# The dense layers' up product by seven block products, with its sums on GpSimd

## The reference, cut to what matters

```python
def sqrelu_mlp(h, w1, w2):              # h (1, 512, 1024), w1 (1024, 4096), w2 (4096, 1024)
    u = jax.nn.relu(jnp.einsum('bsd,df->bsf', h, w1))
    return jnp.einsum('bsf,fd->bsd', u * u, w2)

for i in range(2):
    hn = rmsnorm(h, norm_mix[i])
    mix = conformer_conv(hn, ...) if i == 0 else pool_mixer(hn, ...)
    h = h + mix
    h = h + sqrelu_mlp(rmsnorm(h, norm_mlp[i]), mlp_w1[i], mlp_w2[i])
return rmsnorm(h, final_norm)
```

## Time and profile before

| What | Value |
|---|---|
| Median of 3 runs | 886.83 us (886.45 to 887.8) |
| Span of the profiled execution | 884.7 us |
| Granted TensorE clock | 0.999 of full speed |
| PE busy | 874.4 us (99%) |
| DVE busy | 700.1 us (79%) |
| ACT busy | 464.1 us (52%) |
| POOL busy | 140.0 us (16%) |
| SP's queue | 29.4% of the DMA engines' span |

### The profile page before, as it was taken

How to read it: one execution, slowest core, us unless ns; L and a number is a source line. 1 busy time by engine, 2 the same in 40 slices (tenths; PEclk the granted TensorE clock), 3 DMA queues, 4 the chain that set the end, 5 groups by cost and what they waited for, 6 DMA issues and landing times.

```text
span 884.7 us, 11889 instructions
## 1 busy us (share of the span) xinstructions
PE 874.4 (99%) x4383; PEld 740.7 (84%) x4383; DVE 700.1 (79%) x946; ACT 464.1 (52%) x675; POOL 140.0 (16%) x122
## 2 busy tenths in 40 slices
PE   8999999999999999999999999999999999999997
PEld 8888887899888888888888889988888888888886
DVE  6899999768786968776778788897786968776866
ACT  6898976247272544536273544637272544536243
POOL 1699970560000020000000040000000000000000
PEclk9999999999999999999999999999999999999999
DMA  9766732305413142331314222122313142331202
GB/s 302 198 166 150 188 73 98 143 1 191 143 47 143 57 175 77 118 133 57 142 48 167 77 73 90 48 98 94 142 47 142 52 174 77 125 127 64 72 1 95
DMA packets 49255, 97.62 MB, mean 110 GB/s; under 512 B 1562, under 2 KB 18978, under 8 KB 48324
## 3 DMA queue, kind: packets, MB, share of 16 engines
q1 hardware_dynamic: 48068, 89.54, 29.4%
q0 software_dynamic: 1008, 7.34, 4.0%
q10 hardware_dynamic: 144, 0.26, 0.1%
HBM read 87.70 MB, written 2.10 MB: 101 GB/s over the span
## 4 chain that ended last, share of the span: by engine, by line
PE 95%; DVE 2%; DMA 1%; ACT 1%; issue 0%; SPq 0%; DVEq 0%; ACTq 0%
PE ps L1454 19%; PE ps L1452 19%; PE ps L1453 19%; PE ps L1717 10%; PE ps L1715 10%; PE ps L1716 10%; PE ps L1530 3%; PE ps L1471 1%; PE ps L1629 1%; PE ps L1634 1%; PE ps L1630 1%; DMA h<-in_x 1%; DVE tok L894 0%; DVE act_lo L900 0%; DVE tok L928 0%
## 5 line engine op out<-in xcount | busy, mean ns | idle before, releaser
L1452 PE MATMUL ps<-act_hi,w_hi 128*128 128x512 f32 (+1 forms) x688 | 254.9, 370 | 0.0
L1453 PE MATMUL ps<-act_lo,w_hi 128*128 128x512 f32 (+1 forms) x688 | 254.2, 369 | 0.0
L1454 PE MATMUL ps<-act_hi,w_lo 128*128 128x512 f32 (+1 forms) x688 | 254.2, 369 | 0.0
L1715 PE MATMUL ps<-w_hi,u_hi 128*128 128x512 f32 x392 | 152.7, 390 | 0.0
L1717 PE MATMUL ps<-w_hi,u_lo 128*128 128x512 f32 x392 | 152.7, 390 | 0.0
L1716 PE MATMUL ps<-w_lo,u_hi 128*128 128x512 f32 x392 | 152.5, 389 | 0.0
L685 ACT ACTIVATE relu<-ps 128x512 f32<-128x512 f32 x36 | 21.5, 597 | 242.8 <-PE ps L1454 242.8
L1452 PEld LDWEIGHTS ps<-act_hi,w_hi 128*128 128x128 f32 x688 | 129.7, 188 | 21.8
L1454 PEld LDWEIGHTS ps<-act_hi,w_lo 128*128 128x128 f32 x688 | 129.6, 188 | 21.8
L1453 PEld LDWEIGHTS ps<-act_lo,w_hi 128*128 128x128 f32 x688 | 129.7, 188 | 21.7
L1172 DVE TENSOR_TENSOR w_lo<-w_raw,w_hi 128x1024 fp32r<-128x1024 f32 x70 | 85.1, 1220 | 58.0 <-ACT w_hi L706 58.0
(11 more groups left out here) (237 smaller groups left out, 1264.0 us busy)
## 6 DMA issues: line engine op xcount, KB each, us to landing
w_raw<-in_mlp_w SPq DMA_DIRECT2D x32, 1024.0 KB, 5.0
w_raw<-in_mlp_w SPq DMA_DIRECT2D x16, 2048.0 KB, 8.0
w_raw<-in_conv_w SPq DMA_DIRECT2D x16, 512.0 KB, 5.5
prod_a<-prod_a POOLq DMA_DIRECT2D x7, 1024.0 KB, 7.9
w_raw<-in_conv_w SPq DMA_DIRECT2D x2, 2048.0 KB, 11.0
h<-in_x SPq DMA_DIRECT2D x4, 512.0 KB, 5.8
out<-tok SPq DMA_DIRECT2D x7, 256.0 KB, 2.0
gain<-in_norm_mlp SPq DMA_DIRECT2D x2, 512.0 KB
```

Source lines behind the costliest of these rows:

```text
L1452: nc.tensor.matmul(dst, lh, rh, start=(n == 0), stop=False)
L1453: nc.tensor.matmul(dst, lh, rl, start=False, stop=False)
L1454: return nc.tensor.matmul(dst, ll, rh, start=False, stop=(n == count - 1))
L1715: nc.tensor.matmul(dst, lh, rh, start=(f == 0 and (opens or i not in (0, 5))), stop=False)
```

## The change

The up product of groups 1 to 7 is also done by seven block products. The 1024 channels, the 512 features of the group and the 512 tokens are each cut in two. Weight blocks w11, w21, w12, w22 (128 x 1024 elements per block: 4 channel chunks x 256 features) and four sums v1 to v4 of them give seven weight parts; the activation quarters and four sums z1 to z4 (formed once for a layer, eight steps) give seven right sides. A part is 2 feature tiles x 4 channel chunks x 3 = 24 matmuls of 256 columns. The seven products are put together by seven sums on DVE (sum_two to sum_21), each of one SBUF operand and one PSUM bank, into a11, a12, a21, a22 in SBUF, and relu and square then work in SBUF. ACT copies the first product out of PSUM (copy_one).

Where things are done: POOL forms t1 to t4 (b_sums), v1 to v4 (w_sums) and the activations' sums (mlp_sums), adds acc to h at a layer's end (acc_out), and makes pw_lo; all low parts of weights and activations are on DVE (w_low, mid_low, x_low). High parts stay on ACT. The loads of pool_scale and pool_w are moved behind load_groups(0), that of norm_mix[1] behind the last low part of the layer's activations. The last down product starts on two features' tiles and takes the other two after that.

```diff
--- before.py
+++ after.py
...
+        w_parts = (w11, v1, v2, w12, v3, v4, w22)
+        wp_hi = w1_hi[:].rearrange("p (k c f) -> p k c f", k=4, c=4)
+        wp_lo = w1_lo[:].rearrange("p (k c f) -> p k c f", k=4, c=4)
+        def act_quarter(half, pair):
+            return slice(4 * half, 4 * half + 4), slice(256 * pair, 256 * pair + 256)
+        x_hi = (x_sum[:, 0], x_two[:, 0], x_sum[:, 2], act_hi[:, 0:4, 256:512])
+        x_lo = (x_sum[:, 1], x_two[:, 1], x_sum[:, 3], act_lo[:, 0:4, 256:512])
+        x_parts = (x_raw[:, 1], tok[:, 1, :].rearrange("p (c t) -> p c t", c=4), x_raw[:, 3], act_raw[:, 0:4, 256:512])
+        z1, z2, z3, z4 = x_parts
...
+            def b_sums(layer, g, which, again=True):
+                sums, splits = LAYER_SUMS * layer, LAYER_SPLITS * layer
+                for k in which:
+                    if k == 0:
+                        pool.wait_ge(m2_in[0], 16 * g + 16 * (GROUPS * layer + 1))
+                        if again:
+                            pool.wait_ge(w2_lo_ok, 7 * g + (splits - 2))
+                        into, left, right = t1, b12, b11
+                    elif k == 1:
+                        pool.wait_ge(m2_in[1], 16 * g + 16 * (GROUPS * layer + 1))
+                        into, left, right = t3, b22, b12
+                    elif k == 2:
+                        if again:
+                            pool.wait_ge(w2_lo_ok, 7 * g + (splits - 1))
+                        into, left, right = t2, b22, t1
+                    else:
+                        pool.wait_ge(w2_lo_ok, 7 * g + (splits + 3))
+                        into, left, right = t4, t2, b21
+                    nc.gpsimd.tensor_tensor(into, left, right, ALU.subtract).then_inc(b_sum_ok, 1)
+                    pool.wait_ge(b_sum_ok, 4 * g + (sums + k + 1))
+            def w_sums(layer, g, which, again=True):
+                for k in which:
+                    if k == 0:
+                        pool.wait_ge(w1_in, 16 * g + (32, 16 * (GROUPS + 2))[layer])
+                        into, left, right, op = v3, w11, w21, ALU.subtract
+                    elif k == 1:
+                        if again:
+                            pool.wait_ge(w1_mid_lo_ok, mid_lows(layer, g) - 1)
+                        into, left, right, op = v2, w22, v3, ALU.subtract
+                    elif k == 2:
+                        pool.wait_ge(w1_lo_ok, first_low(layer, g) + 1)
+                        into, left, right, op = v1, v2, w11, ALU.add
+                    else:
+                        pool.wait_ge(w1_mid_lo_ok, mid_lows(layer, g) + 3)
+                        into, left, right, op = v4, w12, v2, ALU.subtract
+                    nc.gpsimd.tensor_tensor(into, left, right, op).then_inc(w_sum_ok, 1)
+                    pool.wait_ge(w_sum_ok, 4 * g + (LAYER_WSUMS * layer - 4 + k + 1))
...
+            def x_block(layer, k, into, half, pair):
+                cs, at = act_quarter(half, pair)
+                x_step(layer, k, into, act_hi[:, cs, at].bitcast(F32), act_lo[:, cs, at].bitcast(F32), ALU.add)
+            def mlp_sums(layer, gen):
+                nc.gpsimd.memset(acc[:], 0.0).then_inc(acc_zero, 1)
+                b_sums(layer, 0, (0, 1, 2), False)
+                pool.wait_ge(act_lo_ok, 4 * gen + NB)
+                x_block(layer, 1, z1, 1, 1)
+                x_block(layer, 2, z3, 0, 1)
+                x_step(layer, 3, z3, z1, z3, ALU.subtract)
+                b_sums(layer, 0, (3,))
+                x_block(layer, 4, z2, 0, 0)
+                x_step(layer, 5, z2, z3, z2, ALU.add)
+                x_step(layer, 6, z1, z1, z2, ALU.subtract)
+                pool.wait_ge(up_mm, LAYER_PARTS * layer + GF)
+                x_block(layer, 7, z4, 1, 0)
+                x_step(layer, 8, z4, z4, z2, ALU.subtract)
+                w_sums(layer, 1, (0, 1, 2), False)
+                w_sums(layer, 1, (3,))
+                b_sums(layer, 1, (0, 1))
+                with pool.Fori(1, MIDDLE - 1) as w:
+                    b_sums(layer, w, (2, 3))
+                    w_sums(layer, w + 1, (0, 1, 2))
+                    w_sums(layer, w + 1, (3,))
+                    b_sums(layer, w + 1, (0, 1))
+                b_sums(layer, MIDDLE - 1, (2, 3))
+                w_sums(layer, MIDDLE, (0, 1, 2))
+                w_sums(layer, MIDDLE, (3,))
+            def acc_out(layer):
+                pool.wait_ge(banks_read, layer + 1)
+                tiles = ((h[:, 2:4, 512:D], acc[:, 0]), (h[:, 0:2, 512:D], acc[:, 0]),
+                         (h[:, 2:4, 0:512], acc[:, 1]), (h[:, 2:4, 512:D], acc[:, 1]))
+                for k, (at, add) in enumerate(tiles):
+                    if k == 3:
+                        pool.wait_ge(acc_out_ok, 4 * layer + 1)
+                    nc.gpsimd.tensor_tensor(at, at, add, ALU.add).then_inc(acc_out_ok, 1)
+            mlp_sums(0, GEN_MLP0)
+            acc_out(0)
...
+            pool.wait_ge(pw_hi_ok, 1)
+            pool.wait_ge(acc_out_ok, 4)
+            nc.gpsimd.tensor_tensor(pw_lo[:], pw_raw, pw_hi[:].bitcast(F32), ALU.subtract).then_inc(pw_lo_ok, 1)
...
+            mlp_sums(1, GEN_MLP1)
+            acc_out(1)
...
+            def w_part(i):
+                nc.scalar.copy(wp_hi[:, i % 4], w_parts[i]).then_inc(w1_hi_ok, 1)
+            def next_parts(layer, g):
+                act.wait_ge(w_sum_ok, 4 * g + (LAYER_WSUMS * layer - 4 + 3))
+                w_part(1)
+                w_part(2)
+                w_part(3)
+            def copy_one(layer, g):
...
-                    relu_square(n, UP_BANK[0], squared[0][:, 0], upper_b)
-                    next_w1(0)
-                    relu_square(n + 1, UP_BANK[1], squared[0][:, 1], diff_b)
-                    act.wait_ge(usq_ok, n + 2)
+                    act.wait_ge(m_done, 14 * w + (tiles - 4))
+                    upper_b()
+                    copy_one(layer, w)
+                    late_parts(layer, w, (4, 5))
+                    diff_b()
+                    late_parts(layer, w, (6,))
+                    lower_b()
+                    act.wait_ge(up_sum_ok, summed + 3)
+                    relu_square(n, a11, a11)
+                    act.wait_ge(usq_ok, n + 1)
-                    lower_b()
+                    act.wait_ge(up_sum_ok, summed + 5)
+                    relu_square(n + 1, a22, a22)
+                    act.wait_ge(up_sum_ok, summed + 6)
+                    relu_square(n + 2, a21, a21)
+                    last_b()
                     act.wait_ge(a_sum_ok, 4 * w + (sums + 1))
                     a_high(1)
-                    next_w1(1)
...
+                    act.wait_ge(up_sum_ok, summed + 7)
+                    relu_square(n + 3, a12, a12)
+                    act.wait_ge(usq_ok, n + 4)
+                    a_high(2)
+                    a_high(3)
+                    next_first()
...
+            def w_low(n, i):
+                dve.wait_ge(w1_hi_ok, n + i + 1)
+                nc.vector.tensor_tensor(wp_lo[:, i % 4], w_parts[i], wp_hi[:, i % 4].bitcast(F32),
+                                        ALU.subtract).then_inc(w1_lo_ok, 1)
+            def mid_low(layer, g, i):
+                dve.wait_ge(w1_hi_ok, first_part(layer, g) + i + 1)
+                nc.vector.tensor_tensor(wp_lo[:, i], w_parts[i], wp_hi[:, i].bitcast(F32),
+                                        ALU.subtract).then_inc(w1_mid_lo_ok, 1)
...
+            def up_sum(layer, g, parts, own, into, left, right):
+                dve.wait_ge(up_mm, first_part(layer, g) + parts)
+                if own:
+                    dve.wait_ge(up_sum_ok, up_sums(layer, g) + own)
+                nc.vector.tensor_tensor(into, left, right, ALU.add).then_inc(up_sum_ok, 1)
+            def sum_two(layer, g):
+                dve.wait_ge(p1_copied, g + ROUNDS * layer)
+                up_sum(layer, g, 3, 0, a12, a11, bank_quarter(0))
+            def sum_four(layer, g):
+                up_sum(layer, g, 3, 1, a21, a12, bank_quarter(3))
+            def sum_11(layer, g):
+                up_sum(layer, g, 4, 1, a11, a11, bank_quarter(1))
+            def sum_three(layer, g):
+                up_sum(layer, g, 5, 2, a12, a12, bank_quarter(0))
+            def sum_22(layer, g):
+                up_sum(layer, g, 5, 4, a22, a12, bank_quarter(3))
+            def sum_12(layer, g):
+                up_sum(layer, g, 6, 2, a21, a21, bank_quarter(1))
+            def sum_21(layer, g):
+                up_sum(layer, g, 7, 5, a12, a12, bank_quarter(2))
...
             def mlp_add(layer, q):
                 dve.wait_ge(m_done, LAYER_TILES * (layer + 1) - NQ + q + 1)
+                if q:
+                    dve.wait_ge(acc_out_ok, 4 * (layer + 1))
                 at = h_tile(q // 2, q % 2)
                 nc.vector.tensor_tensor(at, at, mlp_bank(q), ALU.add).then_inc(m_added, 1)
...
-                    upper_sums()
+                    now = first_part(layer, w)
                     b_low(0)
-                    w1_low(n + 4, 0)
```

(74 more changed lines are left out.)

291 lines of the change are left out of this document (176 added, 115 removed).

## The result

The changed kernel takes **1045.76 us** (median, 1045.49 to 1049.24), the kernel before 886.64 on the same chip: a ratio of 1.180, 95% interval 1.179 to 1.182. 1005 was forecast, with a range up to 1045; the direction and the mechanism came true, the time is 41 too long and 0.8 outside the range. The profiled span is 1043.7 against 884.7, so 159 us are to be accounted for.

A forecast was written before the change was run, and what follows sets the result against it. PE bounds the kernel before; after the change DVE, held by POOL, was to bound rounds. Terms +94, +18, 0, +2, +4 total +118 on span 884.7, 1002.7, plus 2.1 for the median: 1005 us, range 975 to 1045.

The forecast's parts named there:

- PE's starts, the counts of DVE and ACT: Per round: up product 1.6 us shorter, PE 39.2 without waits; DVE 32.8 and ACT about 23 by count.
- The exclusive path: POOL's sums and DVE's two-SBUF-operand instructions can't share one read path, asked for 39.2 us a round; PSUM-reading DVE instructions escape.
- Term (1): Twelve rounds, each going from 40.85 to 48.7 us: +94 us, bounds -20 and +146.
- the walk: One round followed instruction by instruction on each engine: PE waits sum to 9.45 us, round 48.7.
- Term (2): First group of each layer: POOL owes twelve sums after the last act_lo; 9 us per layer, +18, bounds 0 and +28.
- (4): Entry into layer 1: t1 on POOL holds DVE's norm once, +2 us, bounds 0 and +5.
- (5): End of layer 0: POOL and ACT's row of acc_out, scalings, pw_hi, pw_lo gates the first norm at 40; +4 us (0, +8).
- Term (3): Group 7: 1.6 us won and the first two waits lost, net 0, bounds -3 and +5.
- The path does not matter: Rival: POOL's sums don't hold DVE, rounds take 39.65 us, total about 870; chance 0.11.
- Packs better: Rival: POOL's sums fall mostly beside DVE's PSUM-reading instructions, rounds 42 to 46.5 us, total 905 to 975; chance 0.2.
- Worse than walked: Rival: POOL's v1 or t4 becomes late and adds to ACT's chain, rounds over 52 us, total above 1045; chance 0.07.

The follow-up runs named there:

- with clears: Changed kernel with POOL's sums of weights and activations replaced by zero-writing clears, so those sums are left out; 905.05 us.
- experiments 1 to 3: Changed kernel, POOL's sums as clears: 905.05 us; its up, down or all weight sums on DVE: 1024.2, 1033.0, 1000.0; kernel before with idle POOL work: 913.85.
- the kernel with clears and the ends on DVE: Changed kernel with POOL's weight and activation sums as clears, plus the last acc sums and the pooling weights' low part on DVE; 892.75 us.

## Why the prediction was right in kind and 41 us short

- **PE's starts, the counts of DVE and ACT: right.** 39.2 was forecast for a round whose waits are gone; with clears it is 39.86. DVE's 32.8 by count is 33.6.
- **The exclusive path: right**, and shown by experiments 1 to 3. So is which instructions are outside it: DVE's that read PSUM kept 0.68.
- **Term (1), twelve rounds: right in size, in part by luck**, 92.9 for 94. A round in the middle of the loop is 47.7 where the walk gave 48.7; twelve of them would be 82 more than before. Most of the other 11 comes from the two rounds behind the first groups (51.8 and 55.5), which the walk took as like the rest; with clears they take 43.7 and 44.7, where a round in the middle takes 39.9.
- **Term (2), first groups: mis-sized**, 37.3 for 18. The walk took POOL's row as what is late, put its end at 41.7 behind the last act_lo and let the down product finish on time. POOL's row ended 36 behind it, earlier, but the down product took 36.4 and 34.7 instead of 19.1: DVE's low parts and sums, six small ones and two large between 215 and 239, each stood behind a POOL sum (2.8 to 3.4 instead of 0.68 and 1.22). In layer 0's, PE waited 11.5 and, at a granted clock of 0.76 over the stretch, was 5.7 longer at the same matmuls: that makes the 17.3. The prediction has no term for the clock. I had also discounted the walk's 12 to 9, with no row for it.
- **Terms (4) and (5), the junction: mis-sized**, 19.0 for 6. POOL's row began and ended where forecast (15 and 41.6 us into group 7), and the hold at the second norm was there (3.26 for 1.28). What failed is "gate the first norm" at 40: the norm came 49.7 into group 7. DVE's own row of u_lo and w1 low parts, which I had not walked, alternated with POOL's row; its last part, 11.2 for 4.6, ended only at 592, and the last down product, which needs u_lo, was stretched from 16.4 to 28.8. Taking acc_out and pw_lo off POOL gives back 6.3. Of the 9.6 to 9.8 that stay even with the other sums off POOL or left out too, the timelines show where they are, but no run tries them by themselves. In the kernel with clears and the ends on DVE, PE waits 7.7 for the norm's result (0.7 before) and 2.0 for u_lo, and DVE works almost without a gap from the last u_lo (502.02) to the first norm (519.81), 44.8 into group 7 where it was 34.6:

```profile
502.63 4.62 DVE L1443 TENSOR_TENSOR h<-h,acc 128x1024 f32<-128x1024 f32 x4
507.17 6.82 DVE L1335 TENSOR_TENSOR w_lo<-w_raw,w_hi 128x1024 fp32r<-128x1024 f32 x4
...
519.81 1.28 DVE L1111 SCALAR_TENSOR_TENSOR tok<-h,rinv,gain 128x1024 f32<-128x1024 f32 x1
```

In the kernel before, the sums of acc (486 to 494) and pw_lo (497 to 499) stood ahead of the last u_lo (501.9). The scalings and the copy are not what gates there: they end at 507.6, pw_lo begins at 514.0.

- **Term (3): right**, 0.5 a layer for 0 (the up product of group 7 takes 22.3 for 21.8). **The end of layer 1: missed**, 5.6 for nothing. acc_out was priced in layer 0 only. In layer 1 the same four POOL sums hold DVE's u_lo (2.85 and 2.88 for 0.68), and PE waits 5.8 for them in the last down product; on DVE they cost nothing (tail 28.2).
- **Ahead of layer 0: missed**, 3.2 for 0. The three b sums of group 0 (192.13 to 199.44) hold the tiny two-operand instructions of the norm, 2.4 and 2.2 instead of 0.2 each.
- **The rivals.** "The path does not matter" is refuted: without holds the kernel would be near 893 to 905, as far as the kernels with clears stand for it, not 870, since a round gives back only 1.0 of the 1.6 and the junctions cost. "Packs better" did not occur: a round took 47.7, not 42 to 46.5. Its price was also summed too low at one end: with the +24 of terms (2), (4) and (5), rounds of 42 to 46.5 give 925 to 979, not 905 to 975. "Worse than walked" has the right total (above 1045) by luck: no v1 or t4 late on a round's path, but the stretches between rounds.

All in all, the round, where DVE's list was walked instruction by instruction, came out within 3%; the entries and the junction, where only POOL's row was followed, came out at two to three times the forecast, and the last down product of layer 1 had no term at all.

## What to carry to other kernels

Before work moves from DVE to POOL, add DVE's whole time in the stretch, at its solo durations, and the time of all POOL instructions that read SBUF, as measured beside DVE. Where the sum stayed below PE's time it was free here (30.5 + 8.0 beside 40.85). Where it was above, each kernel lost: 30.5 + 16.9 gave 44.95, 37.3 + 9.8 gave 46.6 to 46.8, 32.8 + 21.4 gave 47.7. With the weight sums on POOL the kernel is 46 us longer than with the same sums on DVE. The exclusion costs most where POOL has a long row and DVE many short instructions, since each short one waits for a whole long one (36.4 for a down product of 19.1). Walk the entries and ends of a loop as carefully as the loop.

## What the runs showed of the hardware

- The exclusion alternates one for one: with POOL in a row, DVE gets one instruction in between two sums, whatever its length (0.68 recorded as 2.9, 1.22 as 3.4; POOL's 2.40 as 2.7 and 3.2).
- Clears on POOL are free for DVE (30.50 busy in a round with 12.4 us of them, as without).
- POOL's instruction with one SBUF operand takes part in it (0.96 alone, up to 1.94 beside DVE), and for the same time it costs DVE about the same (7.7 us of it cost 2.7 a round, as 8.0 us with two operands did). The Trainium skill ("SBUF — State Buffer", section "Who interferes with whom") has any GpSimd instruction that reads SBUF contend with a DVE one of two SBUF inputs; the trace agrees.
